# Half of a 31-tap depthwise convolution moved to TensorE in column strips of 32

## What is computed

```python
proj = rmsnorm(h) @ w_in                       # 1024 -> 5136 columns
glu  = proj[..., :1024] * sigmoid(proj[..., 1024:2048])
cconv = causal_dwconv(glu, cbuf, conf_dw_w, conf_dw_b)   # 31 taps, one filter for each channel
a_out = silu(layernorm(cconv))
z    = proj[..., 2048:3072]
xbc  = silu(causal_dwconv(proj[..., 3072:5120], mbuf, ssm_conv_w, ssm_conv_b))   # 4 taps
y    = ssd_scan(...xbc, dt...)                 # 16 heads, 2 chunks of 128 tokens
m_out = groupnorm((y + d_skip * xs) * silu(z))
h = h + concat(a_out, m_out) @ w_out
h = h + hier_moe(rmsnorm(h))                   # 16 experts, top 2
h = h + (p @ w_ple) * sigmoid(rmsnorm(h) @ w_ple_gate)
y = rmsnorm(h)
```

## Time and profile before

| | us |
|---|---|
| median of 3 runs (lowest, highest) | 685.66 (684.06, 685.73) |
| span of the profiled execution, first to last instruction | 679.0 |
| the profiled execution's own whole time | not recorded; the median stands 6.7 above the span |
| mean granted clock of TensorE | 0.954 |
| TensorE, VectorE, ScalarE, POOL busy | 621.5, 322.0, 181.3, 75.1 |

### The profile page before, as it was taken

The page is one execution under the profiler, slowest core; times in us unless marked ns, Lnnn a source line. Parts: engine busy times, 40 slices in busy tenths (PEclk is TensorE's granted clock), DMA queues, the critical chain, the costliest instruction groups (busy, mean ns, idle before and its releaser), DMA issues.

```text
span 679.0 us, 8162 instructions
## 1 busy us (share of the span) xinstructions
PE 621.5 (92%) x3011; PEld 422.6 (62%) x3011; DVE 322.0 (47%) x905; ACT 181.3 (27%) x407; POOL 75.1 (11%) x73
## 2 busy tenths in 40 slices
PE   4999999668797988999699999999999999999994
PEld 3888888556676866888383545454545454545783
DVE  1899779987898992101550040404040404040433
ACT  3212154424745663500220101010101010101423
POOL 2000565221411220200000000000000000000000
PEclk9999999976967997999889999999999999999997
DMA  9843443900532241579205898989898989891001
GB/s 336 373 183 125 146 165 125 107 30 29 169 117 93 94 155 63 187 313 422 89 1 214 336 403 338 401 337 404 334 404 338 403 334 406 336 406 43 1 0 64
DMA packets 22201, 149.80 MB, mean 221 GB/s; under 512 B 2560, under 2 KB 2864, under 8 KB 5664
## 3 DMA queue, kind: packets, MB, share of 16 engines
q1 hardware_dynamic: 19296, 136.39, 50.9%
q0 software_dynamic: 2560, 12.82, 6.3%
q10 hardware_dynamic: 320, 0.27, 0.1%
HBM read 142.34 MB, written 7.13 MB: 220 GB/s over the span
## 4 chain that ended last, share of the span: by engine, by line
PE 74%; DVE 17%; ACT 3%; POOL 2%; issue 2%; DMA 1%; DVEq 0%; ACTq 0%; POOLq 0%
PE ps L952 16%; PE ps L914 11%; PE ps L726 10%; PE ps L860 9%; PE ps L981 8%; PE ps L1007 4%; PE ps L995 4%; DVE cat L1134 3%; DVE prod L1134 3%; PE ps L704 2%; DVE xraw_s L1224 2%; PE ps L927 1%; POOL glu L398 1%; PE ps L776 1%; POOL ring L392 1%
## 5 line engine op out<-in xcount | busy, mean ns | idle before, releaser
L726 PE MATMUL ps<-u,ring 128*128 128x264 f32 x640 | 151.0, 398 | 0.0
L726 PEld LDWEIGHTS ps<-u,ring 128*128 128x128 f32 x640 | 125.3, 197 | 23.1 <-issue 0.9
L952 PE MATMUL ps<-ring,xraw 128*64 128x512 f32 x512 | 111.6, 594 | 1.2 <-ACT xraw L655 1.2
L1422 DVE TENSOR_TENSOR h<-h,ps 128x264 f32<-128x264 f32 x64 | 27.5, 429 | 127.9 <-PE ps L995 127.0
L952 PEld LDWEIGHTS ps<-ring,xraw 128*64 128x64 f32 x512 | 36.4, 137 | 72.0 <-issue 72.0
L914 PE MATMUL ps<-xbc 128*128 128x128 f32 (+1 forms) x432 | 76.2, 305 | 0.0
L914 PEld LDWEIGHTS ps<-xbc 128*128 128x128 f32 (+1 forms) x432 | 58.7, 187 | 15.6
L860 PE MATMUL ps<-cat,ring 128*128 128x264 f32 x256 | 60.4, 397 | 2.8 <-DVE cat L1278 2.8
L860 PEld LDWEIGHTS ps<-cat,ring 128*128 128x128 f32 x256 | 50.1, 196 | 12.2 <-issue 3.2
L981 PE MATMUL ps<-ring,xraw 128*64 128x512 f32 x256 | 56.7, 595 | 0.0
L1134 DVE SCALAR_TENSOR_TENSOR cat<-glu,prm,cat 128x256 f32<-128x256 f32 x105 | 55.9, 532 | 0.0
(11 more groups left out here) (243 smaller groups left out, 646.1 us busy)
## 6 DMA issues: line engine op xcount, KB each, us to landing
ring<-in_w_moe SPq DMA_DIRECT2D x96, 1024.0 KB, 7.9
ring<-in_w_in SPq DMA_DIRECT2D x20, 1024.0 KB, 5.0
ring<-in_w_out SPq DMA_DIRECT2D x8, 1024.0 KB, 5.0
ring<-in_state_s POOLq DMA_DIRECT2D x1, 4096.0 KB, 24.3
out_h_s_out<-ring POOLq DMA_DIRECT2D x8, 512.0 KB, 3.7
ring<-in_w_pleg SPq DMA_DIRECT2D x4, 1024.0 KB, 6.9
h<-in_xT SPq DMA_DIRECT2D x2, 528.0 KB, 4.9
out_yT<-cat SPq DMA_DIRECT2D x4, 264.0 KB, 2.1
```

The source lines that it names most:

```text
L726: ins = mm(ps[:, n % (4 if s < NEARLY else 2), 0:T], wv[:, k, q * P:(q + 1) * P], u[:, k, :], start=(k == 0), stop=(k == KD - 1))
L952: ins = mm(ps[e * CAP:(e + 1) * CAP, gu, :], xg[:, 4 * hf + k, e * CAP:(e + 1) * CAP], wv[:, k, :], start=(hf == 0 and k == 0), stop=(hf = ...
L1422: v.tensor_tensor(h[:, c, :], h[:, c, :], ps[:, SC[q], 0:T], ALU.add).then_inc(sc_added[q], 1)
```

## The change

Four of the eight blocks, 4 to 7, have their prompt convolution on TensorE. VectorE keeps blocks 0, 1, 2; block 3 stays where it was; the sample tokens' convolution stays on VectorE.

For a block, SP stores its GLU rows to DRAM and loads them again four times, each time into 32 partitions and shifted by 8 taps. So partition 32 i + m holds channel 32 q + m, 8 i tokens later, for q = 0 to 3. A 128x32 weight of diagonal pieces (`taps`) applies 4 taps at once, and 8 matmuls at offsets r = 0 to 7 cover the 31 taps of one strip of 32 channels. The four strips write partitions 0, 32, 64 and 96 of bank 4.

```diff
-NEARLY = 14
-AFTER_ITEM = [range(31 + i, 32 + i) for i in range(6)] + [range(37, 39), range(39, 40)]
-Z_SILU = 37
+NEARLY = 16
+AFTER_ITEM = [(), (35,), (36,), (), (37,), (), (38,), (39,)]
+Z_SILU = 38
+PE_CONV = (4, 5, 6, 7)
+SHIFTS = 8
+PE_CONV_AFTER = {12: 4, 13: 5, 15: 6}
...
+            def shift(c):                                    # SP, before the load of slot AT["g", j] + 5
+                j = PE_CONV[c]
+                sp.wait_ge(glu_ready, j + 1)
+                sp.dma_start(glu_rows[c], glu[:, j, :]).then_inc(rows_stored, 16)
+                sp.wait_ge(rows_stored, 16 * (c + 1))
+                rows = glu_rows[c].rearrange("(q m) n -> m q n", q=4)
+                for i in range(4):
+                    sp.dma_start(shifted[c % 2][32 * i:32 * i + 32], rows[:, :, SHIFTS * i:SHIFTS * i + SHIFTED])\
+                        .then_inc(shifted_loaded[c % 2], 16)
...
-            pool.dma_start(state, state_s).then_inc(in_st, 16)
+            pool.dma_start(state[:, 0:STATE_SPLIT], state_s[:, 0:STATE_SPLIT]).then_inc(in_st, 16)
...
-                if j == 6:
-                    new_states(0)
-                    new_states(1)
+            pool.wait_ge(pe_conv_psum, len(PE_CONV))
+            pool.dma_start(state[:, STATE_SPLIT:], state_s[:, STATE_SPLIT:]).then_inc(in_st_late, 16)
...
+            for i in range(4):                               # ScalarE's queue, after root(1), before dt
+                n = min(SHIFTS, KC - SHIFTS * i)
+                for q in range(4):
+                    act.dma_start(tap_rows[32 * i:32 * i + 32, :, q, 0:n],
+                                  w[32 * q:32 * q + 32, :, SHIFTS * i:SHIFTS * i + n]).then_inc(in_taps, 16)
...
+            def evacuate_conv(c):                            # ScalarE, after slots 12, 13, 15 and projection 33
+                j = PE_CONV[c]
+                act.wait_ge(pe_conv_psum, c + 1)
+                a.activation(cat[:, j, 0:NPR], ps[:, 4, 0:NPR], ACT.Identity, bias=par("conv_b", j))\
+                    .then_inc(pe_conv_done, 1)
...
+            def conv(c):                                     # TensorE
+                pe.wait_ge(taps_ready, c + 1)
+                pe.wait_ge(shifted_loaded[c % 2], 64 * (c // 2 + 1))
+                if c:
+                    pe.wait_ge(pe_conv_done, c)
+                for r in range(SHIFTS):
+                    for q in range(4):
+                        ins = mm(ps[32 * q:32 * q + 32, 4, 0:NPR], taps[c][:, q, r, :], shifted[c % 2][:, q, r:r + NPR],
+                                 start=(r == 0), stop=(r == SHIFTS - 1))
+                ins.then_inc(pe_conv_psum, 1)
+            for s in range(NEARLY):
+                project(2 * s)
+                project(2 * s + 1)
+                if s in PE_CONV_AFTER:
+                    conv(PE_CONV.index(PE_CONV_AFTER[s]))
...
+            conv(3)                                          # after the transposes of x
             project(2 * NEARLY + 2)
...
+            def spread_taps(c):                              # VectorE
+                v.tensor_tensor(taps[c], tap_rows[:, c].unsqueeze(3).to_broadcast([P, 4, SHIFTS, 32]),
+                                fold.unsqueeze(1).unsqueeze(1).to_broadcast([P, 4, SHIFTS, 32]), ALU.mult)\
+                    .then_inc(taps_ready, 1)
+            dve.wait_ge(in_taps, 16 * 16)
+            for q in range(4):
...
+                if q < len(DVE_CONV):
+                    conv(DVE_CONV[q], 0, KC)
+                spread_taps(q)
                 conv_x(4 * q)
                 conv_x(4 * q + 2)
-            conv(5, 16, KC)
...
-                conv(j, cuts[0], cuts[1])
                 spread_done(i)
-                conv(j, cuts[1], cuts[2])
                 take(i)
```

More of the change, by code:

```diff
@@ L53 @@
 W_IN_ORDER = [(c[0], int(c[1])) for c in "g0 x0 x1 g1 x2 x3 g2 g3 x4 x5 g4 g5 x6 x7 g6 g7 z0 z1 z2 z3".split()]
-NEARLY = 14
-AFTER_ITEM = [range(31 + i, 32 + i) for i in range(6)] + [range(37, 39), range(39, 40)]
-Z_SILU = 37
+NEARLY = 16
+AFTER_ITEM = [(), (35,), (36,), (), (37,), (), (38,), (39,)]
+Z_SILU = 38
 POOL_CONV = 3
+DVE_CONV = (0, 1, 2)
+PE_CONV = (4, 5, 6, 7)
+SHIFTS = 8
+SHIFTED = NPR + SHIFTS - 1
+GLU = KC + NPR
+PE_CONV_AFTER = {12: 4, 13: 5, 15: 6}
+TAPS_AT = [4096, 5120, 6144, 7168]
+STATE_SPLIT = 4
 NORM_BANK = [None, 4, 0, 4, 5]
@@ L92, in build @@
         warm = sb("warm", [P, 12])
-        glu = sb("glu", [P, KD, KC - 1 + NPR])
+        glu = sb("glu", [P, KD, GLU])
         cat = sb("cat", [P, 2 * KD, T])
@@ L120, in build @@
         part_sum = scratch[:, 14336:14336 + 4 * NPR]
+        taps = [scratch[:, at:at + 1024].rearrange("p (q r m) -> p q r m", q=4, r=SHIFTS) for at in TAPS_AT]
+        tap_rows = cbm[:, 1, 2:4, :].rearrange("p a (b r) -> p (a b) r", r=SHIFTS)[:, 0:4 * len(PE_CONV)]            .rearrange("p (c q) r -> p c q r", q=4)
+        fold = ea[:, 0, 0:32]
+        shifted = [scratch[:, at:at + 4 * SHIFTED].rearrange("p (q n) -> p q n", q=4) for at in (12224, 13284)]
+        glu_rows = nc.dram_tensor("glu_rows", (len(PE_CONV), P, GLU), F32, kind="Internal").ap()
         zs = scratch[:, 12224:12224 + KD * T].rearrange("p (j n) -> p j n", j=KD)
@@ L280, in build @@
         pconv_done = sem("pconv_done")
+        rows_stored = sem("rows_stored")
+        in_taps = sem("in_taps")
+        in_st_late = sem("in_st_late")
+        taps_ready = sem("taps_ready")
+        shifted_loaded = [sem(f"shifted_loaded{i}") for i in range(2)]
+        pe_conv_psum = sem("pe_conv_psum")
+        pe_conv_done = sem("pe_conv_done")
         z_ready = sem("z_ready")
         g_root = sem("g_root")
-        ln_root = sem("ln_root")
         pw_psum = sem("pw_psum")
@@ L311, in _ @@
                 sp.dma_start(h[:, 4 * i:4 * i + 4, :], xT[:, 4 * i:4 * i + 4, :]).then_inc(in_x[i], 16)
+            def shift(c):
[7 more added lines that the diff above has]
+                        .then_inc(shifted_loaded[c % 2], 16)
             for n in range(NWIN + NWOUT):
+                for c, j in enumerate(PE_CONV):
+                    if n == AT["g", j] + 5:
+                        shift(c)
                 if n >= MIXR:
@@ L368, in _ @@
             g.memset(eps[:, :], EPS)
+            g.memset(tap_rows, 0.0)
             g.memset(glu[:, :, 0:KC - 1], 0.0)
-            g.memset(xraw[:, :, 0:KS - 1], 0.0).then_inc(pool_self, 1)
-            pool.wait_ge(pool_self, 1)
+            g.memset(glu[:, :, KC - 1 + NPR:GLU], 0.0)
+            g.memset(xraw[:, :, 0:KS - 1], 0.0).then_inc(consts, 1)
+            pool.wait_ge(consts, 1)
             g.affine_select(out=ident[:, :], in_=ident[:, :], compare_op=ALU.not_equal, fill=1.0, base=0,
@@ L580, in _ @@
             evacuate(2 * NEARLY + 1)
+            evacuate_conv(3)
             evacuate(2 * NEARLY + 2)
@@ L778, in spread_rows @@
                 ins.then_inc(out_sem, 1)
-            for n in range(2 * NEARLY):
-                project(n)
+            def conv(c):
[11 more added lines that the diff above has]
+                project(2 * s + 1)
+                if s in PE_CONV_AFTER:
+                    conv(PE_CONV.index(PE_CONV_AFTER[s]))
             pe.wait_ge(hrow_ready, 1)
@@ L1237, in _ @@
             for i in range(2 * NG):
-                j = 6 + i // 4
-                cuts = [min(8 * (i % 4) + d, KC) for d in (0, 4, 8)]
                 if i == NG:
```

68 lines of the change are left out of this document (34 added, 34 removed).

## The result

The changed kernel takes 687.47 us (median of 20 runs, 686.13 to 691.88), the kernel before 683.33 in 20 runs beside them: ratio 1.0072, 95% interval 1.0054 to 1.0090. It is slower by 0.7%, where I had forecast 682.0 and a gain. The profiled execution's span is 685.7, its own time 687.45.

The account below looks back on a forecast made before the run. TensorE bounds the start, VectorE's convolutions of blocks 5 to 7 the stretch up to W_out. First item 16.4 us later, items 19.2 shorter: -2.8, giving 682.9 with the span-to-median difference, named 682.0; own range 678 to 686, ends 670 to 693.

Parts of the forecast that it names:

- rival 3: TensorE's convolutions: the strips run one after another, 39 us more, 721 us in all; chance 0.04.
- When the first item starts: TensorE's serial work before the items: first item at 171.9 instead of 155.45, 16.4 us later, bounds 13 and 24.
- about 5.5 to the store's landing: Block 6's rows through DRAM: 5.5 us after slot 14 until SP's store lands, within 9 us for the whole trip.
- the bound 5: Upper bound, in us, of TensorE's wait for block 6's shifted copies, put at 2.2 with lower bound 0.
- rival 4: Data late: tap pieces after 34 us, or each DRAM copy 4 us slower; TensorE stops 3 to 8 us, 685 to 690; 0.09.
- The taps' issue on ScalarE: Start of the kernel: sixteen tap loads at 0.45 us each on ScalarE's queue, VectorE's first convolution 2.7 us later.
- The items' stage: First item to W_out: 102.2 us falls to 83, between 79 at full clock and 87 with half-clock stretches.
- VectorE's decode(6), decode(7) and the last gate, 4.0: End of the items: this VectorE work takes 4.0 us, before 4.7 us from the last gate's square to W_out.
- Rival 1: Items at full clock and no wait for block 6's copy: stage 79, total 674 to 676 us; chance 0.24.
- Rival 5: Items: VectorE still sets them because POOL's additions block its instructions; stage 87, total 686 us; chance 0.06.
- Rival 2: Late start not given back, items set by ScalarE and TensorE; decides over 86 us; stage 92, total 692; chance 0.17.
- My step from span to median: Whole kernel: the median of the runs lies 6.7 us above the profiled span of 679.0, and this difference is carried.

Follow-up runs that it names:

- A1: The changed kernel with block 6's convolution moved behind projections 32 and 33 and its copies in an own buffer: 682.38 us, 0.9982 of the kernel before.
- D3: A1 plus eight matmuls with unused results on TensorE behind items 3 and 5: 681.03 us, 0.9959 of the kernel before.
- A4: The changed kernel with POOL's state addition on 128x8 numbers instead of 128x1024, so most of it left out: 680.52 us, 0.9963 of the kernel before.
- E1: D2 with each of POOL's state additions as four instructions of 256 columns: 674.44 us, 0.9874 of the kernel before.
- A2: The changed kernel with each block's store and four loads one w_in slot earlier in SP's queue: 684.07 us, 0.9993 of the kernel before.
- D1: The changed kernel with only blocks 6 and 7 on TensorE, late, copies one slot earlier, 4 and 5 on VectorE: 678.79 us, 0.9922 of the kernel before.
- D2: D1 with the tap loads issued by SP after the first four slots instead of by ScalarE: 677.39 us, 0.9918 of the kernel before.

## Why the prediction was wrong

The mechanism was right in both halves, a later start and a shorter stage of items. Both sizes were off to the bad side, and the forecast gain of 2.8 us was smaller than either error.

**The convolution on TensorE** was right: 3.67 us against 4.0, so four strips do run side by side and rival 3 is false. By 13.8 us for strips one after another, a quarter would be 3.46, and 3.67 is 94% of that. The Trainium skill (TensorE: Matmul & The Clock Gate, its table of practical rules) has 2.38 times for three strips; by 79% of ideal that would be an estimate of 4.4 us, which this trace does not bear out for four.

**When the first item starts** was forecast at +16.4 and is +20.2. The failed step is "about 5.5 to the store's landing", counted from the end of slot 14: it was 8.7, of which 1.6 passed before SP issued the store, as forecast, and 7.06 until it was confirmed, behind a 1 MB load and POOL's store. With 0.7 more for the loads, the wait was 5.64 instead of 2.2 (+3.4). I had listed the bound 5 and not what follows it: after the wait the convolution ran in part at half clock, 5.70 instead of 3.67 (+2.0). The shorter strips give 1.3 back. 3.4 + 2.0 - 1.3 = 4.1, and 3.8 was measured. A1 shows cause and price. This is rival 4 in its second form, copies through DRAM some 4 us slower, with 3 to 8 us of stopped TensorE and 685 to 690: the measured 687.5 lies in its range, and I had given rival 4 only 0.09.

**The taps' issue on ScalarE** was mis-sized, 1.04 instead of 0.45 each, and VectorE's first convolution began at 38.7 instead of 29.5 where I had 2.7 later. It cost nothing: TensorE's projections run without a gap to 110.69, because `products` was not late (it began at 76.66, before at 84.06). Only in D3's execution, whose first projection started at 21.3, was there a gap there, of 1.50.

**The items' stage** was forecast at 83 (19.2 shorter) and is 88.5 (13.7 shorter). By pairs of items it took 16.1, 17.6, 23.6 and 26.5 to the last gate against the 13.5, 18, 21 and 22 laid out for full clock, which with the tail gave 79. The largest miss, 4.5, is in the last pair, and its failed term is "VectorE's decode(6), decode(7) and the last gate, 4.0": from the end of the last copy of C (251.20) to the last gate's square (259.36) it took 8.2. Behind item 7 two of POOL's additions had held VectorE for 4.1 us, one at the carried state and one at `decode`'s reduction, so that it was late with all of this. VectorE's work in the stage was put at about 51 us and was 64.5. In the first and third pair stand a spread at half clock each (1.7 more), and in the third the product of 2.48. I can add three half-clock spreads of the chain (5.1) and the tail's two blocks (4.1) to 79 and get 88.2, but that this meets 88.5 is in part luck: the second pair has such a spread and was still 0.4 shorter than laid out, the product's block and the items' own matmuls at half clock are left out, and D3 got only 1.3 us back from two of the spreads. What is safe: my 83 was a point between a clock term of 0 and one of 8, with 5 us for waits inside the items, VectorE's blocked product among them, and nothing for additions that hold VectorE in the tail, though I took every such block for charged. Rival 1, full clock and no wait, failed in both conditions. (Its "after each present gap the clock fell" was misread too: in the kernel before, the spread at 175.10 took 2.05 after a gap of 2.08.) Rival 5, POOL's additions in VectorE's way with a stage of 87, came nearest in mechanism and number for this stage; I had given it 0.06. Rival 2's point, "over 86 us", was passed, but not through half clock alone. A4 and E1 give the price of the additions: without them the stage is 82.0, with each in four pieces (and two blocks on TensorE) 85.4.

**The sum.** +20.2 - 13.7 = +6.5 on W_out against my -2.8; +6.4 was seen. My step from span to median (6.7) was also wrong: 1.8 belongs to any execution, and the rest was that the profiled execution was a quick one and that the median of three runs (685.7) lay 2.3 above that of twenty. That raised my forecast by 2.3, so 682.0 looks closer to 687.5 than it is: the change of the median was forecast at -2.8 and is +4.1.

What stays open: whether POOL's stores are what holds the rows' confirmation back, as the times in A2, D1, D2 and E1 say (3.9 to 9.2 us, each ending with them), why block 7's rows took 5.1 to 8.0 after those stores had landed, with one 1 MB load ahead, and what the dt matmuls' 3.7 to 6.6 us at the start hang on.

## What to carry to other kernels

Work moved from an engine with slack later to one that is full now must be paid at once and is given back only as far as the next loop allows: move only the part that stands where the receiving engine is idle (here two blocks of four, though their gain beyond the order is not shown), and put more other work behind each round trip through DRAM than it takes (here 8 to 14 us from the store's issue to the first matmul that waited for it). Run a change's order of work by itself as well: here it was a gain that the whole change hid. When the busiest engine of a stage is relieved, look for what stretched its instructions: on the lighter engine those stretches stand on the chain with nothing to hide them, and cutting the other engine's long instruction in pieces takes a part of them out (here 2.7 us of the 6 to 7 that the additions cost).

## What the runs showed of the hardware

Four column strips of 32 ran at 94% of four times the rate that full-width instructions have here (0.223 us for 264 columns). A DMA of 32-byte pieces cost ScalarE's queue 1.04 us to issue with four blocks in it, 0.48 (13 in 6.20 us) with two. A store of 147 KB (143.5 in the profile's units) to DRAM was confirmed to SP after 3.86 us with no large load just ahead of it and after 7.06 with one, and after 7.5 to 9.2 with none ahead but POOL's store of 192 KB, itself 12.5 us on its way, still under way. A POOL addition of 2.4 us held VectorE instructions with two SBUF inputs, a custom reduction among them, to its end; four additions of a quarter let them in between.
